# Moving four modulation chunks and GpSimd's side loads behind the V projection, with warm-up matmuls in the first wait

## The chip, the cores and the metric

The kernel runs on one core of one Trainium2 chip. The metric is the device time of one execution in microseconds, as the median of several runs; the profile is of one more execution.

## What is computed

One layer of a diffusion backbone on 256 tokens of width 1024: 128 context tokens and 128 latent tokens. All weights are float32 and are read once. The reference, cut to what matters here:

```python
sh_m, sc_m, gt_m, sh_f, sc_f, gt_f = split(silu(c) @ w_ada + b_ada, 6)     # "modulation", 6 x 1024
h = rmsnorm(x, g_mix) * (1 + sc_m) + sh_m
u, q, k, v, ga, gb = split(h @ w_in, [512, 1024, 1536, 2048, 3072])
a = pool_mixer(u, w_pool, pool_scale) @ w_pa
o = attention(q, k, v) @ w_pb               # latent tokens: window with bias, and cached kc, vc
x = x + gt_m * ((sigmoid(ga) * a + sigmoid(gb) * o) @ w_out)
h = rmsnorm(x, g_ffn) * (1 + sc_f) + sh_f
x = x + gt_f * moe(h)                       # top 4 of 32 experts; b_up is one of its biases
y = rmsnorm(x, g_final)
```

## The kernel before

It is written by hand for the five engines, with semaphores; each engine runs its own list in order. There are two parts: the mixing part (everything up to the router), then a loop over 32 experts, in pairs.

**Weights.** SP (SyncE) loads the weights of the mixing part in 48 chunks of 1 MB in the order of the list `MIX`: `("first", h, i)` are the shift and scale columns of w_ada, `("ada", m, k)` the other modulation columns (m = 1 and 2, eight chunks each), `("in", j, h)` the column block j of w_in (0 pool, 1 q, 2 k, 3 v, 4 to 7 the gates), then w_pa, w_pb, w_out. Each chunk has a slot in the array `ring` (`place_mixing`); before SP may issue it, the chunk that held the slot before must be used: TensorE counts used chunks in `pro_used`, in the order of `MIX`. SP is strictly in order, so a chunk that waits for its slot holds back all behind it. After the mixing part SP streams the expert weights (line 326) as `moe_free` releases slots; the first releases come from TensorE behind its last branch matmul (line 1329).

**TensorE** in the stretch of the change: projections 0 to 2 (`project`, line 1157), the modulation rows (`modulation`, line 1121), the V projection (`project_v`, line 1173: it waits for both chunks of `in 3`), the pooling matmuls (line 1252), `modulation(2, 7, range(4, KB))`, then the attention scores (`scores`, line 1214). `scores(0)` waits for `row_ready` 4, which VectorE gives when it has copied the modulation rows out of PSUM (`mod_rows`, line 752). Then comes the gate stage: `project_gate(4)` to `project_gate(7)` (lines 1188 to 1190), four units each, with score, transpose and probability work between them (`prob_t`, line 1220). After it come attention output, the branch matmuls (lines 1327 to 1329) and the output projection.

**VectorE** splits h and each unit's weights in a rounded top part and a rest. For h (lines 801 and 804) there is one CAST and one subtraction of 2048 elements per partition; the subtraction waits for the end of `project_v`. Per gate unit, `split(n)` (lines 817 and 820) has two CASTs, then two subtractions of the top part from the weights, all operands in SBUF. `project_gate` waits for `unit_ready` of each unit.

**GpSimd** builds constants, then issues loads of its own (`part_load`, line 347): the cached keys, the position bias and w_pool once `in 1 1` has landed, and, when the bias has been copied (`bias_copied`), the side loads b_up (three times), the cached values, g_ffn, w_router and b_router. Then it masks the bias (lines 424 and 427) and splits b_up in three bfloat16 parts (lines 434 to 440: four CASTs and three subtractions; what the reader will find below as its "split"). ScalarE's `z_out(4)`, the first gate sigmoid, waits for the end of that split (`split_done`), since both use the same memory.

**The first stage**: TensorE transposes the small vectors (line 1114), waits for the first w_ada chunks, takes two (line 1135), transposes x (line 1201), takes two more, and forms the columns (`first_columns`, line 1145); `keep_busy` (line 1128) are matmuls with no use but to keep the engine running, `cleared` (line 1165) writes zeros to PSUM banks for the projections.

Of the kernel before, what the change touches and what calls it, by code (L numbers as in the profile page):

```python
# [33 lines left out]
RING0 = 9  # L34
RING1 = 6
NARROW = 27
# [17 lines left out]
MIX += [("in", 1, 1)] + [("ada", 1, k) for k in range(4, KB)] + [("in", 2, 1)] + [("ada", 2, k) for k in range(4)]  # L54
MIX += [("in", 3, 0), ("in", 3, 1)] + [("ada", 2, k) for k in range(4, KB)]
MIX += [("in", j, h) for j in range(4, 8) for h in range(2)]
MIX += [("pa", 0, h) for h in range(2)] + [("pb", 0, h) for h in range(2)] + [("out", 0, h) for h in range(4)]
# [3 lines left out]
def place_mixing():  # L61

    slots = [c % RING0 if c < NARROW else (c - NARROW) % RING1 for c in range(len(MIX))]
    slots[AT["in", 4, 0]:] = [5, 0, 1, 2, 3, 4, 0, 1, 2, 3, 4, 5, 0, 1, 11, 12]
    before = [max((b for b in range(c) if slots[b] == slots[c]), default=None) for c in range(len(MIX))]
    landed = [2 if key[0] == "first" else 1 for key in MIX]
    return slots, before, [sum(landed[b] for b in range(c + 1) if slots[b] == slots[c]) for c in range(len(MIX))]


def layer_kernel(nc, A_x_prompt, A_x_sample, A_cache_k, A_cache_v, A_c, A_c_ctx, A_w_ada, A_b_ada, A_g_mix,  # L70
# [13 lines left out]
    with ExitStack() as ctx:  # L84
# [260 lines left out]
        def _(pool):  # L345
# [68 lines left out]
            pool.wait_ge(bias_copied, 1)  # L414
            for q in range(3):
                part_load(bup[32 * q:32 * q + 32, :], A_b_up[0], L["bup"])
            part_load(vc.rearrange("p (h d) -> p h d", h=HEADS), A_cache_v[0, 0].rearrange("h l d -> l h d"), L["vc"])
            part_load(gffn, A_g_ffn.to_broadcast([P, D]), L["gffn"])
            part_load(wrt[:, :, :], A_w_router[0].rearrange("(k p) n -> p k n", p=P), L["wrt"])
            part_load(brt[:, :], A_b_router.to_broadcast([P, E]), L["brt"])  # L420
            for r in range(2):
# [9 lines left out]
            pool.sem_inc(bias_ready, 1)  # L431

            pool.wait_ge(L["bup"], 48)
            link(nc.gpsimd.tensor_copy(bparts[:, :], bup[0:96, :]))
# [40 lines left out]
        def _(act):  # L475
# [79 lines left out]
            def pt_out(n):  # L555
                act.wait_ge(PT_done, n + 1)
                bank = (6, 4, 6)[n]
                dst = (PTp, PTs[:, 0], PTs[:, 1])[n]
                for b in range(2):
                    ins = nc.scalar.activation(dst[:, 4 * b:4 * b + 4, :],  # L560
                                               ps[:, bank + b, :].rearrange("p (a b) -> p a b", a=4), ACT.Copy)
                ins.then_inc(PT_read, 1)
# [128 lines left out]
        def _(dve):  # L691
# [56 lines left out]

            def mod_rows(m, bank):
                dve.wait_ge(pro_used, AT["ada", m, KB - 1] + 1)  # L750
                dve.wait_ge(L["bada"], 128)
                V.tensor_tensor(modrow[:, m, :], ps[:, bank, :], bada[:, m - 1, :], ALU.add).then_inc(row_ready, 1)

# [41 lines left out]
            ins.then_inc(pooled_ready, 1)  # L795
            mod_rows(1, 6)

# [25 lines left out]

            mod_rows(2, 7)
            split(0)
# [31 lines left out]
            for n in range(6, 10):  # L857
                split(n)
            normalise(1, Ss, TOK)
            for n in range(10, 16):  # L860
                split(n)
# [243 lines left out]
        def _(pe):  # L1105
# [9 lines left out]

            def modulation(m, bank, ks):

                for kk in ks:
                    w = landed(AT["ada", m, kk])
                    for q in range(4):  # L1120
                        ins = mm(ps[32 * q:32 * q + 32, bank, :], cs[:, kk, :], w[:, q * HALF:(q + 1) * HALF],
                                 start=(kk == 0), stop=(kk == KB - 1))
                    ins.then_inc(pro_used, 1)
# [54 lines left out]
            def project_gate(cc):  # L1178
# [14 lines left out]
                pe.sem_inc(pro_used, 2)  # L1193

            pe.wait_ge(silu_ready, 2)
            first_rows(0, range(2))
            for t in range(2):
                pe.wait_ge(xn_ready, t + 1)
# [5 lines left out]
            pe.wait_ge(const_ready, 3)  # L1204
            first_columns(0)
            keep_busy(4, 1)
            cleared(0)
            pe.wait_ge(xr_ready, 2)
            cleared(4)

            def scores(n, keys, bank):
# [33 lines left out]
            pe.wait_ge(kcT_ready, 1)  # L1245
            modulation(2, 7, range(4))
            project_v()
# [6 lines left out]
            ins.then_inc(pool_done, 1)  # L1254
            modulation(2, 7, range(4, KB))
            pe.wait_ge(z_read, 3)
# [9 lines left out]
            for b in range(4):  # L1266
                ins = tp(ps[:, 6, b * P:(b + 1) * P], kT[:, b, 0:P], ident[:, :])
            ins.then_inc(k_t, 1)
            project_gate(5)
            pe.wait_ge(prob_ready, 1)  # L1270
            pe.wait_ge(knew_ready, 1)
            prob_t(Sp, 6)
            project_gate(6)
            pe.wait_ge(prob_ready, 2)
            prob_t(Ss[:, :, 0:P], 4)
            project_gate(7)
            pe.wait_ge(PT_read, 1)
            prob_t(Ss[:, :, P:TOK], 6)
            def spread(n):

                m, t = n // 2, n % 2
                if n == 0:
                    pe.wait_ge(PT_read, 2)
                    pe.wait_ge(z_read, 8)
# [240 lines left out]
```

## Time and profile before

| | |
|---|---|
| median of three runs | 1195.63 us (1194.5 to 1197.3) |
| the profiled execution's own time | 1197.87 us |
| its span, first to last instruction | 1196.0 us |
| TensorE busy | 1082.1 us, 90% |
| read from HBM | 457.51 MB |
| mean over the span | 384 GB/s |

The busy share of TensorE is large in every part of the span and says little: the expert loop is paced by its transfers, and the mixing part, the first 240 us, by a chain that goes through several engines. What a change in the mixing part is worth has to be read from the waits in that part.

### The profile page before, as it was taken

Reading aid. Unit: us, or ns where it says so; the run is one execution under the profiler, and the core shown is the slowest. Engines: PE = TensorE matmul, PEld = TensorE weight load, DVE = VectorE, ACT = ScalarE, POOL = GpSimd, SP = SyncE. Lnnn points to the kernel's source line nnn. Section 1 sums busy time; section 2 is a strip of 40 time slices with the busy share of each in tenths; the row PEclk is TensorE's granted clock in tenths of the full one; section 3 lists DMA queues with packets and bytes.
Section 4 is the critical chain, followed back from the end, with each engine's and each line's share of the span. In section 5 each row is a group of like instructions: output and inputs, shape, how many; then the busy total and the mean of one; then the engine's idle time right before and its main releaser. Section 6 shows DMA issues by size and latency. Waiting matters only on the chain.

```text
span 1196.0 us, 13483 instructions
## 1 busy us (share of the span) xinstructions
PE 1082.1 (90%) x5379; PEld 523.5 (44%) x5379; DVE 285.6 (24%) x582; ACT 164.4 (14%) x293; POOL 56.2 (5%) x86
## 2 busy tenths in 40 slices
PE   5997999999999999998999899999899889898986
PEld 3753998453333433343434333333334333343332
DVE  3041867332020202020202021211112021303024
ACT  2011424121011101010101011101110111011002
POOL 2137000000000000000000000000000000000000
PEclk9998999999999999999999999999999999999998
DMA  9997563879999999999999999999999999999991
GB/s 328 406 317 283 184 225 117 336 300 429 408 427 428 430 430 427 429 427 427 429 430 430 427 429 429 428 427 429 430 430 427 430 429 427 428 429 430 428 425 42
DMA packets 46869, 459.47 MB, mean 384 GB/s; under 512 B 4429, under 2 KB 4489, under 8 KB 20121
## 3 DMA queue, kind: packets, MB, share of 16 engines
q1 hardware_dynamic: 45592, 455.12, 91.2%
q0 software_dynamic: 1024, 3.29, 1.1%
q10 hardware_dynamic: 224, 0.69, 0.2%
q8 instruction: 17, 0.28, 0.1%
q14 instruction: 12, 0.09, 0.0%
HBM read 457.51 MB, written 1.57 MB: 384 GB/s over the span
## 4 chain that ended last, share of the span: by engine, by line
PE 53%; DMA 31%; DVE 9%; issue 5%; ACT 1%; SPq 1%; DVEq 0%; POOLq 0%; POOL 0%; ACTq 0%
DMA ring<-in_w_up_dram 28%; PE ps L1474 20%; PE ps L1436 15%; PE ps L1157 3%; PE ps L1365 2%; DMA ring<-in_w_in_dram 2%; DVE arena L991 2%; DVE arena L1027 2%; DVE arena L1018 2%; PE ps L1173 1%; PE ps L1461 1%; PE ps L1188 1%; PE ps L1190 1%; PE ps L1189 1%; DVE arena L1029 1%
## 5 line engine op out<-in xcount | busy, mean ns | idle before, releaser
L1436 PE MATMUL ps<-ring,arena 128*64 128x512 f32 x2048 | 459.3, 602 | 33.2 <-DMA ring<-in_w_up_dram 33.0
L1436 PEld LDWEIGHTS ps<-ring,arena 128*64 128x64 f32 x2048 | 159.9, 139 | 311.0 <-issue 306.6
L1474 PE MATMUL ps<-ring,arena 128*64 128x512 f32 x1024 | 238.8, 626 | 4.2 <-ACT arena L661 3.6
L1474 PEld LDWEIGHTS ps<-ring,arena 128*64 128x64 f32 x1024 | 83.1, 145 | 150.5 <-issue 150.5
L980 DVE COPY cur<-tab 128x8 f32 (+1 forms) x17 | 2.9, 171 | 449.1 <-PE ps L1396 449.1
L1016 DVE TENSOR_SCALAR arena<-ps 128x512 f32<-128x512 f32 x32 | 20.6, 686 | 304.3 <-PE ps L1436 304.3
L1396 PEld LDWEIGHTS ps<-arena 128*128 128x128 f32 x528 | 65.9, 196 | 21.8 <-issue 19.2
L1396 PE MATMUL ps<-arena 128*128 128x128 f32 x528 | 69.2, 284 | 1.0 <-DVE arena L984 1.0
L653 ACT ACTIVATE arena<-arena 128x512 f32<-128x512 f32 x32 | 19.6, 630 | 313.2 <-DVE arena L1016 313.2
L1404 PE MATMUL ps<-arena 128*128 128x512 f32 x128 | 59.2, 605 | 0.0
L641 ACT ACTIVATE arena<-ps 128x512 f32<-128x512 f32 x33 | 19.7, 597 | 245.7 <-PE ps L1396 245.7
L666 ACT ACTIVATE arena<-ps 128x512 f32<-128x512 f32 x32 | 17.4, 594 | 233.1 <-PE ps L1474 233.1
L459 POOL COPY selbuf<-sel 96x128 bf16 x16 | 4.6, 291 | 853.7 <-DVE arena L1018 841.7
L1157 PE MATMUL ps<-ring 128*128 128x256 f32 x192 | 42.7, 381 | 0.0
L991 DVE TENSOR_TENSOR arena<-ps,arena 128x512 f32<-128x512 f32 x64 | 40.9, 680 | 0.0
L1451 PE MATMUL ps<-ident,arena 128*128 128x128 f32 x32 | 7.2, 310 | 35.9 <-DVE arena L991 35.9
L1157 PEld LDWEIGHTS ps<-ring 128*128 128x128 f32 x192 | 36.2, 190 | 6.9 <-issue 2.2
L1404 PEld LDWEIGHTS ps<-arena 128*128 128x128 f32 x128 | 23.0, 189 | 35.9 <-issue 35.9
L1188 PE MATMUL ps<-parts 128*128 128x256 f32 x128 | 36.7, 287 | 0.6 <-DVE parts L820 0.6
L1189 PE MATMUL ps<-parts 128*128 128x256 f32 x128 | 36.2, 283 | 0.0
L1190 PE MATMUL ps<-parts 128*128 128x256 f32 x128 | 36.2, 283 | 0.0
L1029 DVE SCALAR_TENSOR_TENSOR arena<-arena 128x512 f32<-128x512 f32 x32 | 34.6, 1080 | 1.1
(227 smaller groups left out, 770.5 us busy)
## 6 DMA issues: line engine op xcount, KB each, us to landing
ring<-in_w_up_dram SPq DMA_DIRECT2D x128, 2048.0 KB, 24.2
ring<-in_w_down_dram SPq DMA_DIRECT2D x64, 2048.0 KB, 24.6
ring<-in_w_in_dram SPq DMA_DIRECT2D x16, 1024.0 KB, 12.5
ring<-in_w_ada_dram SPq DMA_DIRECT2D x16, 1024.0 KB, 15.2
ring<-in_w_ada_dram SPq DMA_DIRECT2D x16, 512.0 KB, 11.8
ring<-in_w_out_dram SPq DMA_DIRECT2D x4, 1024.0 KB, 7.3
ring<-in_w_pa_dram SPq DMA_DIRECT2D x2, 1024.0 KB, 7.3
ring<-in_w_pb_dram SPq DMA_DIRECT2D x2, 1024.0 KB, 9.4
```

Source lines behind the costliest of these rows:

```text
L991: V.tensor_tensor(acc[:, t, c], ps[:, GB + n, :], acc[:, t, c], ALU.add).then_inc(acc_done, 1)
L1018: V.tensor_scalar(hid, ps[:, 2:4, :].rearrange("p a b -> p (a b)"), LIMIT, -LIMIT, ALU.min, ALU.max).then_inc(u_read, 1)
L1027: V.tensor_tensor(sig[:, c], sig[:, c], gate[:, c], ALU.mult).then_inc(glu_ready, 1)
L1029: V.scalar_tensor_tensor(out=gate[:, c].rearrange("q (j p) -> q j p", j=4), in0=hid[:, c].rearrange("q (p j) -> q j p", j=4), scalar=1.0, ...
L1157: ins = mm(ps[:, bank + b // 2, (b % 2) * TOK:(b % 2 + 1) * TOK], w[:, kk % 4, b * P:(b + 1) * P], hTm[:, kk, :], start=False, stop=(kk == ...
L1188: mm(out, w_top[:, n % 2, kk, :], hT_top[:, kk, :], start=(kk == 0), stop=False)
L1189: mm(out, w_top[:, n % 2, kk, :], hT_rest[:, kk, :], start=False, stop=False)
L1190: ins = mm(out, w_rest[:, n % 2, kk, :], hT_top[:, kk, :], start=False, stop=(kk == KB - 1))
L1396: ins = mm(ps[:, GB + b, (j % 4) * P:(j % 4 + 1) * P], h2[:, t, 2 * P * (j // 2) + j % 2:2 * P * (j // 2 + 1):2], oh[:, t, :], start=(t == ...
L1404: mm(ps[:, GB + n, :], woT[:, t, :], yb[:, (n % 2) * HALF:(n % 2 + 1) * HALF], start=True, stop=True).then_inc(scat_done, 1)
L1436: ins = mm(ps[CAP * a:CAP * a + CAP, n, :], xgT[:, h, kk, CAP * a:CAP * a + CAP], w[a][:, at + n * HALF:at + (n + 1) * HALF], start=False, ...
L1474: ins = mm(ps[CAP * a:CAP * a + CAP, YB + n, :], hT[:, f, CAP * a:CAP * a + CAP], w[a][:, (f % 4) * D + n * HALF:(f % 4) * D + (n + 1) * H ...
```

## The change

It has five parts.

1. In `MIX`, the chunks `ada 2 4` to `ada 2 7` move behind `in 4` and `in 5`. TensorE takes two of them between `project_gate(4)` and `project_gate(5)` and two after `project_gate(5)`; before, it took all four between the pooling matmuls and the scores. The modulation of m = 2 is thus summed in two halves: the first half and the bias are added by `mod_rows` where it was, and a second `mod_rows` adds the second half later.
2. The slots are dealt out anew. `in 3 1` now takes slot 5, which `ada 2 1` held, instead of slot 0, which `ada 1 5` held.
3. GpSimd's side loads are issued when `in 3 1` has landed, instead of when the bias is copied; the bias masks come ahead of them. The b_up split stays behind its load.
4. In the first stage 16 matmuls of 128x128 stand in the wait for the first chunk, `cleared` moves into two waits, and `keep_busy` has two matmuls instead of four.
5. `prob_t` uses other banks, and with them some waits change (`spread(0)` waits for the third probability copy instead of the second).

```diff
-MIX += [("in", 3, 0), ("in", 3, 1)] + [("ada", 2, k) for k in range(4, KB)]
-MIX += [("in", j, h) for j in range(4, 8) for h in range(2)]
+MIX += [("in", 3, 0), ("in", 3, 1)] + [("in", 4, h) for h in range(2)] + [("ada", 2, 4), ("ada", 2, 5)]
+MIX += [("in", 5, h) for h in range(2)] + [("ada", 2, 6), ("ada", 2, 7)]
+MIX += [("in", j, h) for j in range(6, 8) for h in range(2)]
...
-    slots = [c % RING0 if c < NARROW else (c - NARROW) % RING1 for c in range(len(MIX))]
-    slots[AT["in", 4, 0]:] = [5, 0, 1, 2, 3, 4, 0, 1, 2, 3, 4, 5, 0, 1, 11, 12]
+    slots = [c % RING0 for c in range(len(MIX))]
+    slots[AT["in", 3, 1]:] = [5, 0, 1, 2, 3, 4, 5, 0, 1, 2, 3, 0, 1, 4, 5, 2, 3, 0, 1, 11, 12]
...
             pool.wait_ge(bias_copied, 1)
-            for q in range(3):
-                part_load(bup[32 * q:32 * q + 32, :], A_b_up[0], L["bup"])
-            part_load(vc.rearrange("p (h d) -> p h d", h=HEADS), A_cache_v[0, 0].rearrange("h l d -> l h d"), L["vc"])
...
             pool.sem_inc(bias_ready, 1)
 
+            c_after = AT["in", 3, 1]
+            pool.wait_ge(pro_loaded[mix_slot[c_after]], 16 * mix_held[c_after])
+            for q in range(3):
+                part_load(bup[32 * q:32 * q + 32, :], A_b_up[0], L["bup"])
...
-            mod_rows(1, 6)
+            mod_rows(1, 6, KB - 1, bada[:, 0, :])
...
-            mod_rows(2, 7)
+            mod_rows(2, 7, 3, bada[:, 1, :])
             split(0)
             split(1)
...
             normalise(1, Ss, TOK)
+            dve.wait_ge(row_ready, 4)
+            mod_rows(2, 7, KB - 1, modrow[:, 2, :])
             for n in range(10, 16):
                 split(n)
...
+            pe.wait_ge(vec_c, 1)
+            for _ in range(16):
+                mm(ps[:, 1, 0:P], ident[:, :], ident[:, :], start=True, stop=True)
             pe.wait_ge(silu_ready, 2)
             first_rows(0, range(2))
+            pe.wait_ge(const_ready, 2)
+            cleared(0)
...
             pe.wait_ge(const_ready, 3)
-            first_columns(0)
-            keep_busy(4, 1)
-            cleared(0)
             pe.wait_ge(xr_ready, 2)
             cleared(4)
+            first_columns(0)
+            keep_busy(2, 6)
...
-            modulation(2, 7, range(4))
+            modulation(2, 7, range(4), last=3)
             project_v()
...
             ins.then_inc(pool_done, 1)
-            modulation(2, 7, range(4, KB))
             pe.wait_ge(z_read, 3)
             pe.wait_ge(row_ready, 4)
             scores(0, kT[:, :, 0:P], 4)
...
+            modulation(2, 7, range(4, 6), first=4)
             project_gate(5)
+            modulation(2, 7, range(6, KB))
             pe.wait_ge(prob_ready, 1)
-            pe.wait_ge(knew_ready, 1)
-            prob_t(Sp, 6)
+            pe.wait_ge(mx_ready, 2)
+            prob_t(Sp, 4)
...
                 if n == 0:
-                    pe.wait_ge(PT_read, 2)
+                    pe.wait_ge(PT_read, 3)
```

TensorE's list ahead of the gate stage, before (the V projection is line 1173, the modulation line 1121, the scores line 1214):

```order
L1157 MATMUL ps<-ring 128x256 x16
L1121 MATMUL ps<-ring 32x512 x16
L1173 MATMUL ps<-ring 128x512 x16
L1252 MATMUL ps<-arena,ring 128x256 x4
L1121 MATMUL ps<-ring 32x512 x16
L1214 MATMUL ps<-ring 128x128 x16
L1188 MATMUL ps<-parts 128x256
```

and now (the same lines are 1161, 1125, 1177, 1260, 1222 and 1192):

```order
L1161 MATMUL ps<-ring 128x256 x16
L1125 MATMUL ps<-ring 32x512 x16
L1177 MATMUL ps<-ring 128x512 x16
L1260 MATMUL ps<-arena,ring 128x256 x4
L1222 MATMUL ps<-ring 128x128 x16
L1192 MATMUL ps<-parts 128x256
```

The sixteen modulation matmuls between pooling and scores are gone from here; eight and eight of them stand in the gate stage.

GpSimd's list from its first loads to the b_up split, before (line 347 issues the loads, 424 and 427 mask the bias, 434 on are the split):

```order
L347 DMA ring<-in_w_pool_dram 128x4x128
L347 DMA arena<-in_b_up_dram 32x2048 x3
L347 DMA ring<-in_cache_v_dram 128x8x64
L347 DMA ring<-in_g_ffn_dram 128x1024
L347 DMA wrt<-in_w_router_dram 128x8x32
L347 DMA brt<-in_b_router_dram 128x32
L424 AFFINE_SELECT ring<-ring 64x8x48
...
L427 AFFINE_SELECT ring<-ring 64x8x48
L434 CAST bparts<-arena 96x2048
```

and now:

```order
L347 DMA ring<-in_w_pool_dram 128x4x128
L418 AFFINE_SELECT ring<-ring 64x8x48
...
L421 AFFINE_SELECT ring<-ring 64x8x48
L347 DMA arena<-in_b_up_dram 32x2048 x3
L347 DMA ring<-in_cache_v_dram 128x8x64
L347 DMA ring<-in_g_ffn_dram 128x1024
L347 DMA wrt<-in_w_router_dram 128x8x32
L347 DMA brt<-in_b_router_dram 128x32
L436 CAST bparts<-arena 96x2048
L438 TENSOR_TENSOR arena<-arena,bparts 32x2048
```

The five kinds of side load, and with them the whole split, now stand behind a wait for the landing of `in 3 1`. VectorE's list between the h split and the scores has not changed: the subtraction for h, `mod_rows`, and the splits of units 0 and 1.

## Rows read from the trace of the kernel before

**Rows 1.** The page: GB/s moved in 40 equal slices of the span.

```profile
GB/s 328 406 317 283 184 225 117 336 300 429 408 427 428 430 430 427 429 427 427 429 430 430 427 429 429 428 427 429 430 430 427 430 429 427 428 429 430 428 425 42
```

**Rows 2.** The chain that ended last: start, length, what.

```profile
72.90 25.18 DMA ring<-in_w_in_dram
98.22 15.77 PE ps L1173 x32
...
115.72 3.62 PE ps L1121 x32
...
148.78 1.06 PE ps L1220 x8
161.51 1.07 PE ps L1220 x8
```

**Rows 3.** SP's timeline, the first expert loads.

```profile
208.12 35.83 SPq L326 DMA_DIRECT2D ring<-in_w_up_dram  x8
```

**Rows 4.** Landing of line 315's issues: at 63.94, at 72.90, and all.

```profile
DMA to landing us min/median/max: 18.1/18.1/18.1
...
DMA to landing us min/median/max: 25.2/25.2/25.2
...
DMA to landing us min/median/max: 4.9/12.7/26.8
```

**Rows 5.** DMA from 82.04 to 98.08 us: GpSimd's queue, packets, MB, share.

```profile
q0 software_dynamic: 438, 1.64, 39.6%
```

**Rows 6.** Stretches of 2 us: busy engines, then clock, DMA share, GB/s.

```profile
92.00:94.00 2.00, 0.00 (x0) 0.00 (x0) 0.55 (x1) 0.00 (x0) 2.00 (x1) 0.50 1.06 361
...
100.00:102.00 2.00, 2.00 (x4) 0.91 (x3) 0.00 (x0) 0.00 (x0) 2.00 (x1) 0.54 1.00 418
```

**Rows 7.** TensorE's timeline; in brackets the idle time before.

```profile
11.16 1.93 PE L1135 MATMUL ps<-ring 128*32 128x512 f32 x8 [7.02 <-DMA ring<-in_w_ada_dram]
...
23.27 1.97 PE L1128 MATMUL ps<-selrow,tri 128*128 128x256 f32 x8
...
83.70 2.78 PE L1121 MATMUL ps<-ring 128*32 128x512 f32 x24
...
134.79 1.16 PE L1214 MATMUL ps<-ring 64*128 64x128 f32 x16
```

**Rows 8.** GpSimd's timeline.

```profile
78.21 1.51 POOL L347 DMA_DIRECT2D arena<-in_b_up_dram x3 [16.30 <-ACT ring L531]
...
89.58 1.88 POOL L434 CAST bparts<-arena 96x2048 bf16<-96x2048 f32 x1 [1.50 <-DMA arena<-in_b_up_dram]
91.55 4.90 POOL L436 TENSOR_TENSOR arena<-arena,bparts 32x2048 f32<-32x2048 f32 x1
...
98.48 4.05 POOL L436 TENSOR_TENSOR arena<-arena,bparts 32x2048 f32<-32x2048 f32 x1
...
108.68 1.88 POOL L440 CAST bparts<-arena 32x2048 bf16<-32x2048 f32 x1
```

**Rows 9.** VectorE's timeline.

```profile
90.14 2.41 DVE L801 CAST parts<-ring 128x2048 fp32r<-128x2048 f32 x1 [14.82 <-PE ps L1121]
114.10 2.29 DVE L804 TENSOR_TENSOR parts<-ring,parts 128x2048 fp32r<-128x2048 f32 x1 [21.55 <-PE ps L1173]
...
119.96 0.75 DVE L817 CAST parts<-ring 128x512 fp32r<-128x512 f32 x2
120.75 1.29 DVE L820 TENSOR_TENSOR parts<-ring,parts 128x512 fp32r<-128x512 f32 x2
...
123.96 1.22 DVE L829 TENSOR_REDUCE small<-ps 128x8 f32<-128x1024 f32 x1
```

**Rows 10.** One GpSimd instruction alone, and beside VectorE at the end.

```profile
239.36 0.55 POOL L395 TENSOR_TENSOR small<-small,mhalf 128x1 f32<-128x1 f32 x1 [14.04 <-DVE small L711]
...
1188.52 1.28 DVE L1084 TENSOR_TENSOR x<-x,arena 128x512 f32<-128x512 f32 x2
1188.68 0.93 POOL L395 TENSOR_TENSOR small<-small,mhalf 128x1 f32<-128x1 f32 x1 [88.69 <-DVE small L711]
```

More of the change, by code:

```diff
@@ L34 @@
 RING0 = 9
-RING1 = 6
 NARROW = 27
@@ L414, in _ @@
             pool.wait_ge(bias_copied, 1)
-            for q in range(3):
-                part_load(bup[32 * q:32 * q + 32, :], A_b_up[0], L["bup"])
-            part_load(vc.rearrange("p (h d) -> p h d", h=HEADS), A_cache_v[0, 0].rearrange("h l d -> l h d"), L["vc"])
-            part_load(gffn, A_g_ffn.to_broadcast([P, D]), L["gffn"])
-            part_load(wrt[:, :, :], A_w_router[0].rearrange("(k p) n -> p k n", p=P), L["wrt"])
-            part_load(brt[:, :], A_b_router.to_broadcast([P, E]), L["brt"])
             for r in range(2):
@@ L431, in _ @@
             pool.sem_inc(bias_ready, 1)
+            c_after = AT["in", 3, 1]
+            pool.wait_ge(pro_loaded[mix_slot[c_after]], 16 * mix_held[c_after])
+            for q in range(3):
+                part_load(bup[32 * q:32 * q + 32, :], A_b_up[0], L["bup"])
+            part_load(vc.rearrange("p (h d) -> p h d", h=HEADS), A_cache_v[0, 0].rearrange("h l d -> l h d"), L["vc"])
+            part_load(gffn, A_g_ffn.to_broadcast([P, D]), L["gffn"])
+            part_load(wrt[:, :, :], A_w_router[0].rearrange("(k p) n -> p k n", p=P), L["wrt"])
+            part_load(brt[:, :], A_b_router.to_broadcast([P, E]), L["brt"])
             pool.wait_ge(L["bup"], 48)
@@ L556, in pt_out @@
                 act.wait_ge(PT_done, n + 1)
-                bank = (6, 4, 6)[n]
+                bank = (4, 6, 4)[n]
                 dst = (PTp, PTs[:, 0], PTs[:, 1])[n]
@@ L747, in _, with mod_rows @@
                 V.tensor_scalar(xn[:, t, :], x[:, t, :], rstd[:, t:t + 1], None, ALU.mult).then_inc(xn_ready, 1)
-            def mod_rows(m, bank):
-                dve.wait_ge(pro_used, AT["ada", m, KB - 1] + 1)
+            def mod_rows(m, bank, last, bias):
+                dve.wait_ge(pro_used, AT["ada", m, last] + 1)
                 dve.wait_ge(L["bada"], 128)
-                V.tensor_tensor(modrow[:, m, :], ps[:, bank, :], bada[:, m - 1, :], ALU.add).then_inc(row_ready, 1)
+                V.tensor_tensor(modrow[:, m, :], ps[:, bank, :], bias, ALU.add).then_inc(row_ready, 1)
             for hf in range(2):
@@ L1114, in _, with modulation @@
             tp(ps[:, 7, 0:VEC], vecs[:, :], ident[0:VEC, 0:VEC]).then_inc(vec_t, 1)
-            def modulation(m, bank, ks):
+            def modulation(m, bank, ks, first=0, last=KB - 1):
                 for kk in ks:
@@ L1121, in modulation @@
                         ins = mm(ps[32 * q:32 * q + 32, bank, :], cs[:, kk, :], w[:, q * HALF:(q + 1) * HALF],
-                                 start=(kk == 0), stop=(kk == KB - 1))
+                                 start=(kk == first), stop=(kk == last))
                     ins.then_inc(pro_used, 1)
@@ L1268, in _ @@
             ins.then_inc(k_t, 1)
+            modulation(2, 7, range(4, 6), first=4)
             project_gate(5)
+            modulation(2, 7, range(6, KB))
             pe.wait_ge(prob_ready, 1)
-            pe.wait_ge(knew_ready, 1)
-            prob_t(Sp, 6)
+            pe.wait_ge(mx_ready, 2)
+            prob_t(Sp, 4)
             project_gate(6)
             pe.wait_ge(prob_ready, 2)
-            prob_t(Ss[:, :, 0:P], 4)
+            pe.wait_ge(knew_ready, 1)
+            pe.wait_ge(row_ready, 5)
+            prob_t(Ss[:, :, 0:P], 6)
             project_gate(7)
             pe.wait_ge(PT_read, 1)
-            prob_t(Ss[:, :, P:TOK], 6)
+            prob_t(Ss[:, :, P:TOK], 4)
             def spread(n):
```

## The prediction

> **What bounds the kernel now.** First the page's slices of the span [rows 1]: from the tenth on they stand at 425 to 430 GB/s, so the expert loop runs at the pace of its transfers, and its length is not touched here. It begins when TensorE has finished the branches: SP issues the first expert chunk at 208.12 us [rows 3]. All that follows is laid out from that moment, so the change is worth what it moves that moment.
>
> Then the chain of waits over the mixing part [rows 2]: `in 3 1` is issued at 72.90 and is on the chain for 25.18 us, then the V projection 15.77 (to 113.99), pooling (to 115.72), four modulation chunks 3.62, then copies, scores and the gate stage. The gate stage is TensorE at full pace: from one probability transpose to the next 161.51 - 148.78 = 12.73 us, less 1.06 for the transpose leaves 11.65 for four units, 2.9 each. VectorE needs 0.75 + 1.29, about 2.05 us for the split of a unit [rows 9], and is just ahead of it. So the reader should see two bounds: transfers up to 98 us, TensorE behind 120 us, and between them the stretch that the change works on.
>
> What delays `in 3 1`? The chunk `ada 2 2`, issued at 63.94, landed 18.1 us later, at 82.04, and `in 3 1`, the third chunk behind it, at 98.08 [rows 4]. Three chunks of 1.05 MB at 428 GB/s [rows 1] are 7.4 us, and here they took 16.0. In between GpSimd's queue moved 1.64 MB and held 39.6% of the DMA engines' time [rows 5], 6.4 us. In this wait TensorE's granted clock fell to 0.50, that is 1.2 of 2.4 GHz, and rose again in the stretch from 100 to 102 us [rows 6].
>
> **The first stage.** The first chunk's matmuls took 1.93 us for 8 records, against 2.78 for 24 of the same shape later [rows 7]: the engine started at half pace. The warm-up may save 1 us, `keep_busy` halved saves 1.0 of 1.97 [rows 7], and `cleared`, four short matmuls that leave the path, something between nothing and those 1.97; I take 0.8. That is 2.8 us at the first projection. The sixteen matmuls themselves lie in the 7.02 us of idle time ahead of the first chunk [rows 7]; at 0.13 each (eight transposes in 1.06 [rows 2]) they are 2.1 us, at half pace 4.3, and even twice that would run on only into the wait for the second chunk. But transfers bind from there to 98 us, so only the slot matters: `in 3 1` is now issued when `ada 2 1` is used, two of the three chunks of the 83.70 row in, at 85.5 without any gain and some 83.6 with it, instead of 72.90. The quickest issue of that line landed after 4.9 us [rows 4]; 85.5 + 4.9 = 90.4, 83.6 + 4.9 = 88.5. The whole first stage is worth between 0 and 0.9 us.
>
> **The V projection.** With the side loads gone from the queue, three chunks behind 82.04 land at 82.04 + 7.4 = 89.5 us, 8.6 earlier. Before, it ran at half clock from 98.22 to about 101.9 (the mean of 0.54 puts the rise near the end of that stretch [rows 6]), which cost 1.85 of its 15.77; at full clock it takes 13.9 and ends at 103.4. TensorE still idles some 4 us ahead of it; if that costs the clock again, it ends at 105.3. Before, it ended at 113.99 [rows 2]. Pooling adds 1.7. The 3.62 us of modulation no longer stand before the scores, but they come back in the gate stage, where TensorE is the bound: moved, not saved.
>
> **What is moved beside it.** The side loads are now issued at 89.8 instead of 78.21, and the split of b_up began 11.4 us after the first issue [rows 8]: now at 101.2. Before, the split ran from 89.58 to 110.56, with the 114.10 and 119.96 rows of VectorE behind it and only one VectorE instruction beside it [rows 8, 9]. Now it lies on the h subtraction and the splits of the first gate units, the work that TensorE waits for.
>
> What that costs can be read from the one meeting. VectorE's CAST began at 90.14, while GpSimd's CAST ran to 91.46, and took 2.41 us, of which 1.09 lie behind GpSimd's end; 2048 elements at the pace of the 0.75 row (2 x 512) would be at most 1.5. So it stood still until GpSimd was done. GpSimd's next one then took 4.90 instead of 4.05: it stood still until 92.5. [rows 8, 9] At the kernel's end, a GpSimd instruction that takes 0.55 alone took 0.93 beside two back-to-back TENSOR_TENSORs of VectorE with both operands in SBUF, as the splits' subtractions have; it ended 0.41 us after the first of the two, and before the second [rows 10]. So these wait for each other also, and whoever waits comes in between two instructions that follow each other. The rows thus say: one instruction at a time, in turns.
>
> The Trainium skill, page "SBUF — State Buffer", section "Who interferes with whom", has this as a rule: VectorE's copies and casts in a two-port mode, and its instructions with two SBUF inputs against a GpSimd one that reads SBUF, need a port pair that is locked for a whole instruction. By that rule the sum below stands; were the bandwidth only shared, the two engines would stretch each other by their overlap alone, and the sum would be that of rival (b), near nothing. The trace agrees with the lock (2.41 and 4.90 us).
>
> In turns, by these durations: GpSimd 101.2 to 103.1 (CAST) and 103.2 to 107.2 (subtraction). The h subtraction, 2.29 [rows 9], asked for at 103.4 (or 105.3: no difference then), runs 107.2 to 109.5. `mod_rows`, 0.7 like half of the 1.29 row, reads PSUM and one operand in SBUF, and I take it as free: to 110.2; scores, two sets of 1.0 to 1.16 each (the third set's row [rows 7]), to 112.4. GpSimd CAST to 111.4; VectorE's first CAST of unit 0 to 111.8; GpSimd to 115.9; second CAST to 116.3; GpSimd to 118.2; first subtraction to 118.9; GpSimd to 123.0; second subtraction to 123.7, and unit 0 is ready; GpSimd's last CAST to 125.6. Unit 1 is ready at 127.6. Then the row maximum and the bias, 2.6 (1.22 [rows 9], 0.1, and two reads of PSUM like the 1.29 row), the splits of units 2 and 3 at 2.05 each: 134.3, and TensorE, 2.9 per unit and waiting for each, ends `project_gate(4)` at about 137.9. Before, the work behind it began at 134.79 [rows 7]. That is +3.2; the modulation adds 3.6; waits of some 0.3 in the later gates, which TensorE's later start covers, come off. The remaining edits: `spread(0)` now waits for one more copy, 0 to 0.3; the second `mod_rows`, 0.69, lies in VectorE's slack ahead of unit 10. If the clock falls in TensorE's 11 us of idle time, unit 0 runs slow while unit 1 isn't ready anyway. Sum: +6.3 to +6.6. I take +6.5.
>
> **The rivals.** (a) *The engines don't get in each other's way* at this place: the h subtraction runs 103.4 to 105.7, scores to 108.5, `project_gate(4)` to 120.3 instead of 134.8; with 3.6 back, -10.5 us, and -8.6 if the clock falls. For it: all the transfers are early enough (`in 4 1` would land by 101 even with all side loads ahead of it, 89.5 + 4.9 + 6.4). Against it: both meetings above. Place: the first splits; it decides for faster wherever GpSimd's split costs VectorE under some 7 us of the path. 1185 to 1187 us. (b) *Only part of it*: VectorE's subtractions don't wait, or its two CASTs and two subtractions each go as one turn. Then unit 0 is ready at 109 to 118, and the sum is -5 to +4; the kernel ends between 1191 and 1200, 1196 as likely as any. Against it: the 0.93 row, where GpSimd came in between two subtractions. (c) *The split comes yet later*, because b_up lands 4 us later among the new chunks than the 11.4 us of before say: GpSimd then meets more unit splits, +8 to +10, 1204 to 1206.
>
> **How the numbers follow.** The sum goes against the profiled execution, 1197.87 us (span 1196.0); the median of the runs is 1195.63, 2.2 lower, and a shift is the same for both: 1195.63 + 6.5 = 1202.1. Turns with their own scatter (the split 3 us earlier or later against the V projection: +2.5 to +9) and (c) together 0.60, with 1198 to 1206 as their own range; (a) 0.21; (b) 0.19. Faster or slower by 0.2%, 2.4 us, is about what a measurement of this kernel can tell. From (b) I give 0.08 to faster, 0.06 to same, 0.05 to slower; from the turns 0.03 to same. Faster 0.29, same 0.09, slower 0.62. The range leaves out half of (a), 0.11, and 0.05 above: 1186 to 1206.
>
> **What would show it.** The V projection starts at 89 to 91 us instead of 98.22: right about the transfers. GpSimd's first split CAST near 101; the h subtraction takes over 4 us instead of 2.29; CASTs of VectorE's first splits take 2 to 4 us where they took 0.4; TensorE idle for some 11 us before unit 0 near 123; the first expert load at 214 to 215. If the h subtraction takes 2.3 us beside a running GpSimd and unit 0 is ready before 110, the turns are wrong and (a) holds: first expert load at 198. If the V projection starts later than 92, the step on the slot of `in 3 1` is wrong.

## The result, and the profile after

The changed kernel takes 1204.24 us (median of 4 runs, 1200.92 to 1205.68), the kernel before, measured beside it, 1196.47 us (4 runs, 1194.50 to 1198.21): ratio 1.0067, 95% interval 1.004 to 1.0094. It is slower, by 7.8 us of the medians; the forecast was 1202.1.

The moment from which the expert loop is laid out comes first. SyncE's timeline of the changed kernel, its first expert loads:

```profile
214.63 4.25 SPq L326 DMA_DIRECT2D ring<-in_w_up_dram  x4
```

It was 208.12 [rows 3]: 6.5 us later. TensorE's timeline around the V projection and at the end of `project_gate(4)`; in brackets the idle time before:

```profile
89.35 15.67 PE L1177 MATMUL ps<-ring 128*128 128x512 f32 x32 [3.93 <-DMA ring<-in_w_in_dram]
104.86 1.89 PE L1260 MATMUL ps<-arena,ring 128*128 128x256 f32 x8
111.14 3.79 PE L1222 MATMUL ps<-ring 64*128 64x128 f32 x32 [4.39 <-DVE arena L754]
123.52 0.55 PE L1192 MATMUL ps<-parts 128*128 128x256 f32 x1 [8.59 <-DVE parts L822]
...
137.81 1.16 PE L1222 MATMUL ps<-ring 64*128 64x128 f32 x16
139.49 1.92 PE L1125 MATMUL ps<-ring 128*32 128x512 f32 x16
```

The V projection starts 8.9 us earlier than in [rows 2], but the work behind `project_gate(4)` begins at 137.81 instead of 134.79 [rows 7]. In between TensorE waits twice for VectorE, 4.39 and 8.59 us. VectorE's timeline says what it did there:

```profile
105.13 5.26 DVE L806 TENSOR_TENSOR parts<-ring,parts 128x2048 fp32r<-128x2048 f32 x1 [18.42 <-PE ps L1177]
110.32 0.68 DVE L754 TENSOR_TENSOR arena<-ps,gtf 128x512 f32<-128x512 f32 x1
110.92 1.50 DVE L819 CAST parts<-ring 128x512 fp32r<-128x512 f32 x1
112.34 4.28 DVE L819 CAST parts<-ring 128x512 fp32r<-128x512 f32 x1
116.65 2.26 DVE L822 TENSOR_TENSOR parts<-ring,parts 128x512 fp32r<-128x512 f32 x1
118.83 4.54 DVE L822 TENSOR_TENSOR parts<-ring,parts 128x512 fp32r<-128x512 f32 x1
123.30 2.44 DVE L819 CAST parts<-ring 128x512 fp32r<-128x512 f32 x2
125.77 1.29 DVE L822 TENSOR_TENSOR parts<-ring,parts 128x512 fp32r<-128x512 f32 x2
```

and GpSimd's timeline in the same stretch, the split of b_up:

```profile
102.21 1.89 POOL L436 CAST bparts<-arena 96x2048 bf16<-96x2048 f32 x1 [8.28 <-DMA arena<-in_b_up_dram]
104.19 4.06 POOL L438 TENSOR_TENSOR arena<-arena,bparts 32x2048 f32<-32x2048 f32 x1
108.31 3.83 POOL L440 CAST bparts<-arena 32x2048 bf16<-32x2048 f32 x1
112.22 4.12 POOL L438 TENSOR_TENSOR arena<-arena,bparts 32x2048 f32<-32x2048 f32 x1
116.40 1.97 POOL L440 CAST bparts<-arena 32x2048 bf16<-32x2048 f32 x1
118.45 4.38 POOL L441 TENSOR_TENSOR arena<-arena,bparts 32x2048 f32<-32x2048 f32 x1
122.89 2.23 POOL L442 CAST bparts<-arena 32x2048 bf16<-32x2048 f32 x1
```

Read the two lists together. The h subtraction asks at 105.13, GpSimd's subtraction ends at 108.25, and 2.1 us later, at 110.39, the h subtraction is done; GpSimd's CAST, asked for at 108.31, ends 1.75 us behind that. The second CAST of unit 0 ends 0.28 us behind GpSimd's subtraction (116.62 and 116.34), the second subtraction of unit 0 0.54 us behind the next one (123.37 and 122.83). Only `mod_rows` (line 754, one operand in PSUM) keeps its 0.68 us beside a running GpSimd CAST. Unit 0 took two CASTs and two subtractions from 110.92 to 123.37, 12.4 us, where [rows 9] have 2.08 (119.96 to 122.04).

The chain of waits of the changed kernel goes from the transfer of `in 3 1` through the V projection to VectorE's splits, and from the last branch matmul into the expert loop:

```profile
83.76 5.46 DMA ring<-in_w_in_dram
...
89.35 15.68 PE ps L1177 x32
...
214.76 22.56 PE ps L1376 x52
```

and from the page, the transfers, again at 428 or 429 GB/s from the twelfth slice on:

```profile
GB/s 333 405 338 246 147 222 143 301 280 416 417 428 429 429 428 428 429 429 428 429 429 429 429 429 429 429 428 429 429 429 429 429 429 429 429 429 429 429 428 84
```

### The profile page after: what moved, and what is told of

Read it like the earlier page. It is cut to its first block, busy times and chain, and to the rows that moved or that the text cites. A ratio compares the mean times of both kernels' runs of the same rounds, so it can differ in the third digit from the quotient of the medians.

```text
span 1199.0 us, 13542 instructions
## 1 busy us (share of the span) xinstructions
PE 1085.1 (91%) x5407; PEld 531.7 (44%) x5407; DVE 300.5 (25%) x583; ACT 164.6 (14%) x293; POOL 58.0 (5%) x86
## 4 chain that ended last, share of the span: by engine, by line
PE 53%; DMA 29%; DVE 10%; issue 5%; SPq 1%; ACT 1%; DVEq 0%; POOL 0%; ACTq 0%
DMA ring<-in_w_up_dram 28%; PE ps L1485 20%; PE ps L1447 15%; PE ps L1161 4%; PE ps L1376 2%; DVE arena L995 2%; DVE arena L1031 2%; DVE arena L1022 2%; PE ps L1177 1%; PE ps L1472 1%; PE ps L1192 1%; PE ps L1194 1%; PE ps L1193 1%; PE ps L1125 1%; DMA ring<-in_w_ada_dram 1%
## 5 line engine op out<-in xcount | busy, mean ns | idle before, releaser
L1192 PE MATMUL ps<-parts 128*128 128x256 f32 x128 | 37.5, 293 | 9.0 <-DVE parts L822 9.0
L1193 PE MATMUL ps<-parts 128*128 128x256 f32 x128 | 37.0, 289 | 0.0
L1194 PE MATMUL ps<-parts 128*128 128x256 f32 x128 | 37.0, 289 | 0.0
```

Source lines behind the costliest of these rows:

```text
L1192: mm(out, w_top[:, n % 2, kk, :], hT_top[:, kk, :], start=(kk == 0), stop=False)
L1193: mm(out, w_top[:, n % 2, kk, :], hT_rest[:, kk, :], start=False, stop=False)
L1194: ins = mm(out, w_rest[:, n % 2, kk, :], hT_top[:, kk, :], start=False, stop=(kk == KB - 1))
```

## The experiments

Ten kernels ran. "First expert load" is the issue of the first chunk by SyncE, in the profiled run of each; it leaves out the loop, which adds 986 to 990 us (the last section). It comes from one trace per kernel: where nothing kept TensorE's clock up, the V projection alone took between 15.55 us (e4) and 17.04 (e2), so a difference of about 1 us at this marker is not resolved. Ratios are to the kernel before, measured beside each.

| kernel | first expert load | work behind `project_gate(4)` starts | median, ratio (95%) |
|---|---|---|---|
| before | 208.12 | 134.79 | 1 |
| changed | 214.63 | 137.81 | 1204.24, 1.0067 (1.004 to 1.0094) |
| e4 first stage alone | 207.93 | 134.51 | 1197.82, one run |
| e3 changed, side loads back | 208.87 | 132.05 | 1197.82, 1.0019 (1.0009 to 1.0028) |
| e2 side loads alone | 212.87 | 139.55 | 1201.17, 1.0043 (1.0029 to 1.0057) |
| e1 b_up early | 206.50 | 129.68 | 1196.13, 1.0003 (0.9994 to 1.0012) |
| e5 b_up back, rest late | 206.35 | 129.54 | 1194.31, 0.9977 (0.9967 to 0.9987) |
| e6 = e5 kept warm | 202.88 | 126.06 | 1192.91, 0.997 (0.9958 to 0.9982) |
| e7 changed, kept warm | 214.34 | 137.51 | 1204.19, one run |
| e8 changed, shorter split | 212.62 | 135.81 | 1202.47, 1.0051 (1.0031 to 1.0071) |
| e9 changed, no split | 200.44 | 123.62 | 1190.53, 0.9952 (0.994 to 0.9964) |
| e10 = e6, unit 0 before h | 201.55 | 124.74 | 1189.78, 0.9948 (0.9935 to 0.9961) |

**The parts alone: e2, e3, e4.** e2 is the kernel before with only this moved behind the masks (the same lines as in the diff of the change):

```diff
+            c_after = AT["in", 3, 1]
+            pool.wait_ge(pro_loaded[mix_slot[c_after]], 16 * mix_held[c_after])
             for q in range(3):
                 part_load(bup[32 * q:32 * q + 32, :], A_b_up[0], L["bup"])
...
```

> The kernel before with nothing but the side loads (and with them the split) moved behind the landing of in 3 1. Theory: V projection from about 89.5 to 105, the split meets the h subtraction and the first unit splits as in the changed kernel, project_gate(4) ends near 137.5; the four modulation chunks stay ahead of the scores and are hidden under VectorE's delay, so the gate stage isn't longer: first expert load at 211 (before 208.1, changed 214.6), ratio to before 1.002. Rival (no turns, the modulation is the price): 205 or earlier, ratio 0.997.

e3 is the changed kernel with

```diff
             pool.wait_ge(bias_copied, 1)
+            for q in range(3):
+                part_load(bup[32 * q:32 * q + 32, :], A_b_up[0], L["bup"])
...
-            c_after = AT["in", 3, 1]
-            pool.wait_ge(pro_loaded[mix_slot[c_after]], 16 * mix_held[c_after])
-            for q in range(3):
...
```

> The changed kernel with the side loads back where they were. Theory: in 3 1 lands near 98 again, V projection ends at 113.5, scores 3 us earlier than before since no modulation stands ahead of them, project_gate(4) ends near 130.5, the gate stage is 3.7 us longer: first expert load at 207.7, the same time as before within 1 us (ratio 0.9995). No long instructions of VectorE. Rival (the modulation chunks between the gates cost more than their own 3.7 us): 211 or later.

e4 is the kernel before with the edits of the first stage:

```diff
+            pe.wait_ge(vec_c, 1)
+            for _ in range(16):
+                mm(ps[:, 1, 0:P], ident[:, :], ident[:, :], start=True, stop=True)
...
-            keep_busy(4, 1)
...
+            keep_busy(2, 6)
```

> The kernel before with the first-stage edit alone (warm-up matmuls, clearing in waits, two keep_busy). Theory: the first projection starts 2.7 us earlier (26.1 to 23.4), but transfers bind up to the V projection, which starts at 98 as before; first expert load at 208.1 within 0.5 us. Rival (it carries through): V projection and first expert load 2.7 us earlier.

The side loads' move alone costs 4.8 us, the modulation's move with the first stage and the new slots 0.8, the first stage nothing (-0.2). e2 and e3 came out 1.9 and 1.2 us later than expected (212.87 against 211, 208.87 against 207.7). In e2 VectorE and GpSimd meet as in the changed kernel; its timeline of VectorE:

```profile
106.96 3.67 DVE L806 TENSOR_TENSOR parts<-ring,parts 128x2048 fp32r<-128x2048 f32 x1 [19.48 <-PE ps L1175]
...
113.83 5.00 DVE L819 CAST parts<-ring 128x512 fp32r<-128x512 f32 x2 [0.92 <-DMA ring<-in_w_in_dram]
118.86 6.72 DVE L822 TENSOR_TENSOR parts<-ring,parts 128x512 fp32r<-128x512 f32 x2
```

e3 shows the modulation's account: the first gate is done 2.7 us earlier (132.05 against 134.79), and from there to the first expert load it takes 76.8 us, where before and e2 take 73.3 and every kernel with the moved modulation 76.8. So 3.5 us come back in the gate stage. Before, the four chunks' 3.64 us were not all on the path: VectorE waited for them only 2.97 us, ahead of `mod_rows`:

```profile
119.36 0.69 DVE L752 TENSOR_TENSOR arena<-ps,gtf 128x512 f32<-128x512 f32 x1 [2.97 <-PE ps L1121]
```

**What the split costs: e9.** The changed kernel with this edit in GpSimd's list:

```diff
-            link(nc.gpsimd.tensor_copy(bparts[:, :], bup[0:96, :]))
-            for q in (1, 2):
...
-            nc.gpsimd.tensor_copy(bparts[64:96, :], bup[64:96, :]).then_inc(split_done, 1)
+            nc.gpsimd.tensor_copy(bparts[:, :], bup[0:96, :]).then_inc(split_done, 1)
```

> The changed kernel with GpSimd's b_up split left out but for its first CAST, so the two lower bfloat16 parts of b_up are not computed; transfers and all other work as in the changed kernel. Theory (the split beside VectorE is the whole loss): the h subtraction takes 2.3 us right behind the V projection (105.1 to 107.4), unit 0 ready near 110.1, first expert load near 200 instead of 214.6, about 1188 us (ratio 0.993). Rival (part of the loss is in late weights or in the new order of the gate stage): first expert load at 204 or later.

It leaves out two of the three parts of b_up, so it only prices the split; it is no kernel to use.

VectorE's timeline in e9:

```profile
105.59 2.29 DVE L800 TENSOR_TENSOR parts<-ring,parts 128x2048 fp32r<-128x2048 f32 x1 [18.54 <-PE ps L1171]
107.80 0.68 DVE L748 TENSOR_TENSOR arena<-ps,gtf 128x512 f32<-128x512 f32 x1
108.40 0.75 DVE L813 CAST parts<-ring 128x512 fp32r<-128x512 f32 x2
109.19 1.29 DVE L816 TENSOR_TENSOR parts<-ring,parts 128x512 fp32r<-128x512 f32 x2
```

The h subtraction and unit 0 have their durations of [rows 9] back, with the same transfers and the same order on the other engines. Unit 0 is ready at 110.5 instead of 123.4, and the first expert load is 14.2 us earlier. The split beside VectorE is the loss, and more than the whole of it; the rival would have left the load at 204 or later. One more wait goes with the split, ScalarE's `z_out(4)` for `split_done`; it didn't bind in the changed kernel, where the split ended at 125.12 and the gate that ScalarE reads only at 137.8.

**A shorter split: e8.** The changed kernel with

```diff
-                link(nc.gpsimd.tensor_tensor(brem[32 * q:32 * q + 32, :], bup[32 * q:32 * q + 32, :],
-                                             bparts[32 * q:32 * q + 32, :], ALU.subtract))
+            link(nc.gpsimd.tensor_tensor(brem[0:96, :], bup[0:96, :], bparts[0:96, :], ALU.subtract))
```

once, ahead of the loop.

> The changed kernel with one of GpSimd's b_up split subtractions fewer: the first two are computed as one instruction over 96 partitions, which takes 4.05 us out of the split's 21. Theory (one instruction at a time, in turns): VectorE's casts and subtractions for the first two units meet one GpSimd instruction fewer, unit 0 ready near 122, unit 1 near 124 instead of 127.1, first expert load near 211.6 instead of 214.6, about 1201 us. Rival (the units are late for another reason): first expert load unchanged at 214.6.

GpSimd's timeline in e8:

```profile
103.31 1.89 POOL L436 CAST bparts<-arena 96x2048 bf16<-96x2048 f32 x1 [8.76 <-DMA arena<-in_b_up_dram]
105.28 4.06 POOL L437 TENSOR_TENSOR arena<-arena,bparts 96x2048 f32<-96x2048 f32 x1
109.41 5.86 POOL L439 CAST bparts<-arena 32x2048 bf16<-32x2048 f32 x2
```

and VectorE's:

```profile
106.58 4.91 DVE L805 TENSOR_TENSOR parts<-ring,parts 128x2048 fp32r<-128x2048 f32 x1 [19.14 <-PE ps L1176]
...
123.38 1.29 DVE L821 TENSOR_TENSOR parts<-ring,parts 128x512 fp32r<-128x512 f32 x2
```

One instruction fewer made units 0 and 1 ready at 122.3 and 124.7 instead of 123.4 and 127.1. From the end of the h subtraction to unit 1 it took 13.2 us instead of 16.7, 3.5 less. The load came only 2.0 us earlier, not 3, because b_up landed later in this run: the split began at 103.31 instead of 102.21, and the h subtraction was done 1.1 us later (111.49 against 110.39). The V projection ended 1.5 us later too (106.47 against 105.02), but by e7 its end doesn't set the turns. The direction and most of the size are those of the turns.

**Is TensorE's clock on the path? e7.** The changed kernel with, ahead of `project_v()`,

```diff
+            pe.wait_ge(row_ready, 3)
+            keep_busy(6, 6)
```

> The changed kernel plus matmuls of no use on TensorE in its wait ahead of the V projection. Theory (the h subtraction waits for GpSimd's subtraction to end at 108.2 us, not for TensorE): V projection 1.9 us shorter, and the first expert load unchanged, 214.6 within 0.4 us. Rival (TensorE is still the path there): first expert load 1.9 us earlier.

Stretches of 2 us of the changed kernel (busy engines, then the granted clock as a share of 2.4 GHz, DMA share, GB/s):

```profile
90.00:92.00 2.00, 2.00 (x4) 0.72 (x3) 0.00 (x0) 0.00 (x0) 2.00 (x5) 0.50 1.04 385
92.00:94.00 2.00, 2.00 (x4) 0.86 (x3) 0.00 (x0) 0.00 (x0) 1.94 (x3) 0.65 1.15 410
```

and of e7:

```profile
90.00:92.00 2.00, 2.00 (x6) 0.88 (x5) 0.00 (x0) 0.00 (x0) 2.00 (x4) 1.00 1.06 388
```

e7's TensorE, VectorE and GpSimd on the timeline, one fence each:

```profile
89.23 13.97 PE L1177 MATMUL ps<-ring 128*128 128x512 f32 x32 [1.50 <-DMA ring<-in_w_in_dram]
```

```profile
103.31 2.88 DVE L806 TENSOR_TENSOR parts<-ring,parts 128x2048 fp32r<-128x2048 f32 x1 [17.08 <-PE ps L1177]
106.72 3.68 DVE L819 CAST parts<-ring 128x512 fp32r<-128x512 f32 x1
```

```profile
102.16 1.89 POOL L436 CAST bparts<-arena 96x2048 bf16<-96x2048 f32 x1 [8.33 <-DMA arena<-in_b_up_dram]
104.13 5.98 POOL L438 TENSOR_TENSOR arena<-arena,bparts 32x2048 f32<-32x2048 f32 x1
```

The V projection is 1.7 us shorter and the load stays (214.34 against 214.63), as the theory said, but not for its reason, which was that the h subtraction waits for GpSimd's subtraction to end at 108.2. The h subtraction now asked at 103.31, ahead of GpSimd's subtraction, and waited only for the CAST (to 104.05); the subtraction waited instead (5.98 us), and the first CAST of unit 0 behind it (3.68 us). The h subtraction gained 4.2 us and unit 0 was ready at 119.2 instead of 123.4, but unit 1 at 126.8 instead of 127.1: the last turn ends where GpSimd's list ends, and that sets the gate.

**The split ahead of the V projection's end: e1, e5, e6.** e1 is the changed kernel with the b_up loads behind w_pool, the split behind the masks, and the other side loads behind the split and `in 3 1`:

```diff
             part_load(wpool, A_w_pool[0].rearrange("g c d -> c g d"), L["wpool"])
+            for q in range(3):
+                part_load(bup[32 * q:32 * q + 32, :], A_b_up[0], L["bup"])
```

> The changed kernel, but b_up is loaded right behind w_pool and split right behind the bias masks; the other side loads are issued when in 3 1 has landed and the split is done. Theory (turns between GpSimd's split and VectorE): the split runs from about 81 to 102 us, ahead of the h subtraction. in 3 1 lands 2 to 3 us later than in the changed kernel (0.79 MB more ahead of it), V projection from 91.5 to 107.2, h subtraction 2.3 us long, unit 0 ready near 112 instead of 125.7 (its second subtraction's end in the changed kernel: 123.4), project_gate(4) ends at 124 instead of 137.8, first expert load at 201 instead of 214.6: about 1190.5 us, ratio to before 0.995. Rival (the modulation chunks in the gate stage or the late transfers are what costs): unit 0 still ready near 120 or the gate stage longer by more than 3.7 us, first expert load at 208 or later, 1196 us or more.

The load came 5.5 us later than expected (206.50 against 201), though the h subtraction (2.29 us) and unit 0 are short again. TensorE's timeline:

```profile
79.15 8.69 PE L1161 MATMUL ps<-ring 128*128 128x256 f32 x32 [5.10 <-DMA ring<-in_w_in_dram]
...
95.86 15.67 PE L1177 MATMUL ps<-ring 128*128 128x512 f32 x32 [4.46 <-DMA ring<-in_w_in_dram]
```

The early loads held up `in 2 1` (landed at 79.10; 73.60 in the changed kernel), with it the use of `ada 2 1`, the slot, and the issue of `in 3 1` (89.75; 83.76 in the changed kernel). It landed at 95.73 instead of 89.22. The median is what the rival gave (1196 us), but its signs aren't there: unit 0 was ready at 116.5, and the gate stage took the 76.8 us of every kernel with the moved modulation. The loads must not go there. e5 has them at their old place (the other side loads and the split as in e1):

```diff
             pool.wait_ge(bias_copied, 1)
+            for q in range(3):
+                part_load(bup[32 * q:32 * q + 32, :], A_b_up[0], L["bup"])
             for r in range(2):
```

> The changed kernel with the three b_up loads back where they were issued before (when the bias is copied, ahead of the masks), and the other side loads left late, behind in 3 1. The split follows its load. Theory (turns between GpSimd's split and VectorE's h subtraction are the loss): three b_up loads in the queue cost in 3 1 about half of what all side loads cost, so it lands near 94 us and the V projection ends near 109.7; the split lies at about 86 to 107 us, clear of the h subtraction, which takes 2.3 us again; unit 0 ready near 114.6, end of the first gate near 127.8, first expert load near 204.6 us, about 1194.5 us (ratio 0.999). Rival (the loss is in the late transfers themselves or in the new slot order, not in the split): no gain on the changed kernel, first expert load stays at 214, 1204 us.

and e6 is e5 with the two lines of e7:

> As the kernel with b_up early and the rest late, plus matmuls of no use on TensorE in its wait ahead of the V projection. Theory (TensorE's granted clock falls in that wait and costs the V projection about 1.9 us, and with the split out of the way the V projection sets the path): V projection 13.8 us instead of 15.7, first expert load 1.9 us earlier than in that kernel, near 202.7, ratio 0.997. Rival (something else ends the wait of the gate stage): V projection shorter, first expert load unchanged.

The V projection and the h subtraction in e5:

```profile
94.50 16.91 PE L1177 MATMUL ps<-ring 128*128 128x512 f32 x32 [3.58 <-DMA ring<-in_w_in_dram]
```

```profile
111.51 2.29 DVE L806 TENSOR_TENSOR parts<-ring,parts 128x2048 fp32r<-128x2048 f32 x1 [16.40 <-PE ps L1177]
```

and the V projection in e6:

```profile
93.95 13.97 PE L1177 MATMUL ps<-ring 128*128 128x512 f32 x32
```

In e5 `in 3 1` landed at 94.36, as expected, but the V projection took 16.91 us and ended at 111.4 instead of 109.7, and the load came at 206.35 instead of 204.6. TensorE had waited 3.58 us ahead of it. e5 leaves nothing out, and with the split ahead of the h subtraction it is 8.3 us earlier at the marker than the changed one. In e6 the V projection took 13.97 us and the load came at 202.88: with the split out of the way the V projection is on the path, and the same two lines that gave nothing in e7 give 3.5 us at the marker, 2.9 of them in the V projection (the medians differ by only 1.4). Some of the 2.9 is chance: the same projection, also behind a wait, took 15.67 us in the changed kernel, e1 and e9.

**A version faster than both: e10.** e6 with e8's edit and, in VectorE's list,

```diff
-            dve.wait_ge(pro_used, AT["in", 3, 1] + 1)
-            V.tensor_tensor(hT_rest, hTm, hT_top.bitcast(F32), ALU.subtract).then_inc(hT_split, 1)
...
             mod_rows(2, 7, 3, bada[:, 1, :])
             split(0)
+            dve.wait_ge(pro_used, AT["in", 3, 1] + 1)
+            V.tensor_tensor(hT_rest, hTm, hT_top.bitcast(F32), ALU.subtract).then_inc(hT_split, 1)
             split(1)
```

> The kernel with b_up early, the rest late and TensorE kept warm, with two more edits: one GpSimd subtraction fewer in the split (so that it ends near 105 us), and VectorE's mod_rows and the split of unit 0 ahead of the h subtraction, in its wait for the V projection. Theory (behind the V projection the path is VectorE's h subtraction, mod_rows and first unit, 5.0 us, beside 3.5 of TensorE's own): scores start at once behind pooling, unit 0 starts near 111.7 instead of 113.25, first expert load near 201.3 instead of 202.9, about 1191.3 us (ratio 0.9957). Rival (in turns with the rest of GpSimd's split the unit's split runs past the end of the V projection and holds the h subtraction back): no gain, ratio 0.997.

VectorE's timeline in e10:

```profile
99.64 4.75 DVE L816 CAST parts<-ring 128x512 fp32r<-128x512 f32 x2 [6.82 <-DMA ring<-in_w_in_dram]
104.43 2.86 DVE L819 TENSOR_TENSOR parts<-ring,parts 128x512 fp32r<-128x512 f32 x2
108.38 2.29 DVE L826 TENSOR_TENSOR parts<-ring,parts 128x2048 fp32r<-128x2048 f32 x1 [1.10 <-PE ps L1176]
110.59 0.76 DVE L816 CAST parts<-ring 128x512 fp32r<-128x512 f32 x2
```

Unit 0 still meets the split (4.75 and 2.86 us), but in time that VectorE has: it is done 1.10 us before the h subtraction starts behind the V projection. The two edits weren't run apart. The first expert load is at 201.55, the kernel 0.5% faster than before and about 1.2% faster than the changed one (0.9948 / 1.0067, from two sets of runs).

## Why the prediction was right

**The transfers.** `in 3 1` issued at 83.6 to 85.5 and landed at 89.5 was the forecast; it was issued at 83.76 and landed at 89.22.

**The first stage.** TensorE's timeline at the first projection, before:

```profile
26.14 4.15 PE L1157 MATMUL ps<-ring 128*128 128x256 f32 x18
```

and after:

```profile
6.14 6.38 PE L1201 MATMUL ps<-ident 128*128 128x128 f32 x32 [1.83 <-DVE cT L735]
...
23.50 6.81 PE L1161 MATMUL ps<-ring 128*128 128x256 f32 x27
```

The projection starts 2.6 us earlier (forecast 2.8), but the price of the warm-up was wrong: sixteen matmuls of 128x128 are 32 records and took 6.38 us, not 2.1 to 4.3. They ended at 12.5, behind the 11.16 at which the first chunk's matmuls had started; those then took 1.92 us for 16 records instead of 1.93 for 8, so the pace made up for the late start. e4 gives 0.2 us at the marker, but with the old slots and side loads. What the first stage is worth in the changed kernel, where the issue of `in 3 1` waits for TensorE, wasn't run.

**The V projection.** Of the two ends given, 103.4 and 105.3, it was the second (105.02): the clock was at 0.50 again behind a wait of 3.93 us. That this makes no difference to the marker was a step of the sum, and e7 shows it (214.34 against 214.63). The reason given there fails: in e7, with the V projection done at 103.2, the h subtraction went ahead of GpSimd's subtraction instead of waiting for it, and what stayed the same was the end of GpSimd's list, 125.15 against 125.12. The scores took 3.79 us at a granted clock of 0.50 (e9: 2.06), so TensorE's last idle stretch ahead of unit 0 was 8.59 us, not some 11; nothing waited for them.

**The turns.** Forecast and measured: the h subtraction done at 109.5 and 110.4, unit 0 ready at 123.7 and 123.4, unit 1 at 127.6 and 127.1, the work behind `project_gate(4)` at 137.9 and 137.8. Each is one instruction at a time, in the order forecast. That the times agree within 0.3 us from unit 0 on is partly luck: the h subtraction was done 0.9 us late, and from there unit 0 took 13.0 us instead of 14.2, since each turn is 0.1 to 0.2 us shorter than the working had it. The split began 1.0 us later than forecast (102.21, since b_up landed at 102.16), a part of rival (c), without effect on the order. e9 prices the whole mechanism at 14.2 us; the forecast had 6.5 + 8.6 = 15.1 between it and rival (a) with a fallen clock. Rival (a) had the right account of everything else: e9 puts it at 7.7 us less than before, where the working said 8.6. (Its first figure, -10.5, doesn't follow from its own times: 120.3 - 134.8 + 3.6 is -10.9.)

The rule of the Trainium skill, page "SBUF — State Buffer", section "Who interferes with whom", that the shared ports are locked for a whole instruction, holds in these rows: waits end where the other engine's instruction ends, and `mod_rows`, with one operand in SBUF, ran through. By shared bandwidth GpSimd's subtraction at 104.19, overlapped for 3.1 us by the waiting h subtraction, would have been stretched; it took 4.06 us, as alone.

**The modulation.** Moved, not saved: 3.5 us in the gate stage against 3.6. The parts that cost 4.8 and 0.8 alone cost 6.5 together, 0.9 more than their sum. The rows say where: the modulation's move brings the first gate forward by 2.7 us with the old side loads (134.79 to 132.05), but only by 1.7 with the late ones (139.55 to 137.81), and it costs 3.5 in both. In e2 unit 0 waits for `in 4` behind the four chunks (0.92 us, the e2 row above) and is ready 2.2 us later than in the changed kernel (125.6 against 123.4), but unit 1, which comes behind the last turn in both, only 0.9 us later (127.9 against 127.1). With one trace of each, 0.9 us is at the limit of what can be told.

**The size.** At the marker the sum is met, +6.5 against +6.5. The medians differ by 7.8; the forecast was 1202.1 from a base of 1195.63, the base measured beside the change was 0.8 higher, and 1.3 us remain that no row accounts for. The loop's scatter is larger than that (the last section), and the interval of the ratio is 4.8 to 11.2 us; that the 1.3 lie there is likely, not shown.

## What to carry to other kernels

When a load is moved, move the work behind it in your head too, and lay that engine's list beside the lists that run there. Here the change without the split's meeting gained nearly 8 us (e9), and the split that followed its load took 14. In these kernels GpSimd work with operands in SBUF wants a stretch in which VectorE waits anyway (its wait for the V projection), and it is worth shortening by instructions, not by partitions. A repair of the clock pays only where TensorE ends the wait: the same two lines gave nothing in e7 and were on the path in e6.

## What the runs showed of the hardware

- Who goes first is decided by who asks first, and that can flip with 2 us: in the changed kernel the h subtraction waited 3.1 us for GpSimd's subtraction; in e7, asked for at 103.31 instead of 105.13, it waited 0.7 for the CAST, and GpSimd's subtraction waited for it (5.98 us instead of 4.06).
- A GpSimd subtraction over 96 partitions takes 4.06 us (e8), over 32 partitions 4.05 [rows 8].
- The three b_up loads are 32 x 2048 x 4 bytes each, 0.79 MB, 1.8 us at 428 GB/s; in e1 they put `in 2 1` back by 5.5 us, in e5 `in 3 1` by 5.1 (94.36 against 89.22, both issued at 83.8). GpSimd's queue held 13.9% of the DMA engines' time from 76 to 100 us in e5, 3.3 us, for 0.79 MB, so about twice the time of its bytes; where the rest of the 5.1 comes from, and whether the 32 partitions are the reason, wasn't tried.
- From the first expert load to the end of the run it takes between 986.1 us (e1) and 990.2 (e3) in the profiled runs, with the same code and loads; the changed kernel's profiled run is one of the short ones (1200.92 - 214.63 = 986.3; before 1197.87 - 208.12 = 989.8). Most of that difference arises at the end: up to the issue of the last eight w_up chunks it takes 879.3 us before and 879.1 in the changed kernel (issued at 1087.42 and 1093.68), and from there to the end 110.5 and 107.2. What makes it stays open, and it is why the whole time of one run says less than the marker.
